# A recurrent block between two FFNs on eight cores: ScalarE functions grouped by channel block, GeLU as one operation, new stage order on TensorE, output weights loaded into freed buffers

## The reference

```python
def rglru_block(h, w_in, conv_w, conv_b, w_a, b_a, w_x, b_x, lam, w_out):
    xb, gate = jnp.split(h @ w_in, 2, axis=-1)
    xb = causal_depthwise_conv(xb, conv_w, conv_b)      # width 4, frames t-3..t
    r = jax.nn.sigmoid(block_diag_linear(xb, w_a, b_a)) # 16 blocks of 64 x 64
    i = jax.nn.sigmoid(block_diag_linear(xb, w_x, b_x))
    log_a = -LRU_C * r * jax.nn.softplus(-lam)
    a = jnp.exp(log_a)
    mult = jnp.sqrt(-jnp.expm1(2.0 * log_a))
    u = mult * (i * xb)
    _, hseq = lax.associative_scan(_lru_combine, (a, u), axis=1)
    y = hseq * jax.nn.gelu(gate)
    return y @ w_out
```

## Time and profile before

| | |
|---|---|
| time before, median of 3 runs | 3065.8 us (2877.21 to 3173.42) |
| the profiled execution | 2881.14 us, its span on the slowest core 2879.6 us |
| spans of the 8 cores in it | 2866.5 to 2879.6 us |
| TensorE, busy share of the span | 91% |
| VectorE / ScalarE / GpSimd | 45% / 28% / 11% |
| table loads of ScalarE | 41, 1283 ns each |

### The profile page before, as it was taken

One profiled execution on the slowest core, in us unless ns is written; L12 is line 12 of the kernel. 1 busy time (PEld: TensorE's weight loads), 2 busy tenths in 40 slices (PEclk: granted clock), 3 DMA queues, 4 the chain that ended last, 5 costly groups with the idle time before them and its releaser, 6 DMA issues.

```text
span 2879.6 us, 31123 instructions; the slowest of 8 cores (2866.5 to 2879.6 us)
## 1 busy us (share of the span) xinstructions
PE 2631.3 (91%) x12224; PEld 1101.3 (38%) x12224; DVE 1282.5 (45%) x2019; ACT 796.7 (28%) x1147; POOL 329.9 (11%) x340
## 2 busy tenths in 40 slices
PE   5999999788888889999998999999677769999999
PEld 1444444333333234444443444444233323444443
DVE  3234434655555451443345234434678734324444
ACT  4110111355565441001114110012377712110100
POOL 0000000011111000000000000000055610000000
PEclk9999999899999989999998999999889979999999
DMA  5412122010001032212212221121011023121213
GB/s 144 77 31 37 30 45 33 8 30 16 16 19 23 15 52 37 37 27 40 45 23 44 37 37 30 30 44 23 4 21 26 2 52 52 30 42 32 37 30 117
DMA packets 56099, 105.88 MB, mean 37 GB/s; under 512 B 4624, under 2 KB 5776, under 8 KB 55952
## 3 DMA queue, kind: packets, MB, share of 16 engines
q0 software_dynamic: 44288, 83.90, 17.7%
q1 hardware_dynamic: 11664, 19.99, 2.3%
HBM read 179.37 MB, written 8.39 MB: 65 GB/s over the span
## 4 chain that ended last, share of the span: by engine, by line
PE 83%; ACT 8%; DVE 5%; issue 1%; DMA 1%; POOL 1%; SPq 0%; ACTq 0%; DVEq 0%; POOLq 0%
PE ps L288 83%; ACT arena L297 6%; DVE arena L300 3%; ACT L297 1%; DVE arena L304 1%; DMA arena<-xT 1%; POOL arena L304 0%; DVE arena L573 0%; DMA arena<-lru_wout 0%; ACT ps L297 0%; DVE arena L718 0%; SPq L326 0%; DVE arena L308 0%; POOL arena L782 0%; DVE arena L311 0%
## 5 line engine op out<-in xcount | busy, mean ns | idle before, releaser
L288 PE MATMUL ps<-arena 128*128 128x512 bf16 (+6 forms) x12224 | 2631.3, 380 | 244.8 <-ACT arena L297 139.4
L288 PEld LDWEIGHTS ps<-arena 128*128 128x128 bf16 (+2 forms) x12224 | 1101.3, 101 | 1774.3 <-issue 275.0
L297 ACT ACTIVATE arena<-ps 128x512 bf16<-128x512 f32 (+5 forms) x680 | 444.9, 661 | 1774.9 <-PE ps L288 1733.7
L304 DVE TENSOR_TENSOR arena<-arena,ps 128x512 bf16<-128x512 bf16 x352 | 242.0, 687 | 956.1 <-PE ps L288 956.1
L300 DVE SCALAR_TENSOR_TENSOR arena<-ps,arena 128x512 f32<-128x512 f32 (+3 forms) x688 | 503.2, 732 | 220.9 <-PE ps L288 219.1
L297 ACT ACTIVATE arena<-arena 128x512 bf16<-128x512 f32 (+4 forms) x338 | 250.1, 756 | 230.0 <-PE ps L288 127.3
L304 POOL TENSOR_TENSOR arena<-arena 128x512 bf16<-128x512 f32 (+2 forms) x112 | 180.6, 1616 | 475.6 <-PE ps L288 266.8
L300 DVE SCALAR_TENSOR_TENSOR arena<-arena,ps 128x512 bf16<-128x512 f32 (+1 forms) x224 | 167.5, 810 | 76.1 <-ACT ps L297 51.5
L439 POOL DMA_DIRECT2D arena<-ffn_win x88 | 62.5, 712 | 1209.0 <-PE ps L288 1208.1
L304 DVE TENSOR_TENSOR arena<-arena 128x512 bf16<-128x512 bf16 (+3 forms) x188 | 87.3, 476 | 94.5 <-ACT arena L297 92.6
L445 POOL DMA_DIRECT2D arena<-ffn_wout x88 | 47.3, 550 | 509.2 <-PE ps L288 508.5
(11 more groups left out here) (20 smaller groups left out, 78.9 us busy)
## 6 DMA issues: line engine op xcount, KB each, us to landing
arena<-ffn_win POOLq DMA_DIRECT2D x88, 512.0 KB, 5.3
arena<-ffn_wout POOLq DMA_DIRECT2D x88, 256.0 KB, 6.5
arena<-xT SPq DMA_DIRECT2D x32, 256.0 KB, 9.5
outT<-arena SPq DMA_DIRECT2D x32, 256.0 KB, 2.9
arena<-attn_win POOLq DMA_DIRECT2D x8, 768.0 KB, 8.5
arena<-lru_win POOLq DMA_DIRECT2D x8, 512.0 KB, 5.4
arena<-bias_tab SPq DMA_DIRECT2D x8, 256.0 KB, 2.9
arena<-attn_wout POOLq DMA_DIRECT2D x8, 256.0 KB, 4.5
```

What stands on the lines that cost most here:

```text
L288: self.P.op("pe", lambda e: e.matmul(out_ap, lhsT, rhs, start=start, stop=stop), reads=reads, writes=[self.ps_t[bank]])
L297: self.P.op("act", lambda e: e.activation(out=out, in_=in_, func=func, **kw), reads=reads, writes=writes)
L304: self.P.op(eng, lambda e: e.tensor_tensor(out=out, in0=in0, in1=in1, op=op), reads=reads, writes=writes)
```

## The change

GeLU becomes one ScalarE operation (`GELU(k)`, function Gelu_apprx_tanh) that reads the gate banks; the Square, one of the Tanh and two VectorE operations of each unit go. The gate projection (`A2`, now `GM(k)`) has two pairs of banks (2,3 and 4,5), and may be issued in halves; `XB` has only banks 0,1. Where `B_rest` handled one unit, the loop now handles both units of a channel block: four Exp in a row, then two Sqrt, and the two GELU a block later beside the Tanh of the next one. The scans and the products with the GeLU come one block later, among the next block's stages. 13 buffers of 128x1024 float32 are dealt out as rings (xc 2, thx 4, Ab 3, tha 4). The GeLU is kept in the norm's scratch and in the unused ends of two weight slots.

At the start, the norm of frame tile 3 is no longer computed before the block, but after `XB(0)`, `GM(0)` and `CONV(0)`. At the end, w_out is loaded in five parts: row 0 early, rows 1 to 4 into weight slots that are done, rows 5 to 7 into two `thx` buffers after the last product of POOL that uses them. The output projection of tile 0 runs rows 0 to 6 for all 8 banks, then row 7 for all; tiles 1 to 3 use four banks in turn. The built program has 33 table loads in place of 41.

```diff
-        if t >= 1:
+        if t >= 1 and not (nn == 4 and t == NT - 1):
             self.rmsnorm_tile(nn, t - 1)
-        if t == NT - 1:
+        if t == NT - 1 and nn != 4:
             self.rmsnorm_tile(nn, t)
...
+        for nm, cnt in (("xc", 2), ("thx", 4), ("Ab", 3), ("tha", 4)):
+            RING[nm] = pool_[k0:k0 + cnt]
...
+        def GELU(k):
+            i = k % 2
+            self.act(gw[i], g2[i], AF.Gelu_apprx_tanh, GB[i], gw_t[i])
...
-            self.act(gw, g2, AF.Square, GB, [Tt["gw"]], scale=0.21145921)
-            self.stt(gw, gw, 1.0, g2, ALU.add, ALU.mult, [Tt["gw"]] + GB, [Tt["gw"]])
-            self.act(gw, gw, AF.Tanh, [Tt["gw"]], [Tt["gw"]], scale=0.7978845608)
-            self.stt(gw, gw, 1.0, g2, ALU.add, ALU.mult, [Tt["gw"]] + GB, [Tt["gw"]])
...
+        XB(0)
+        GM(0)
+        CONV(0)
+        self.rmsnorm_tile(n, 3, 4, 5)
+        BD(0)
+        GM(1, (0,))
+        XB(1)
+        GM(1, (1,))
...
+        for c in range(NCH + 1):
+            u0, u1 = 2 * c, 2 * c + 1
+            if c > 0:
+                GELU(u0 - 2)
+            if 0 < c < NCH:
+                BD(u0)
+            if c > 1:
+                GM(u0 - 1, (1,))
+            if c > 0:
+                GELU(u0 - 1)
+                if c + 2 < NCH:
+                    load_w(c + 2)
+            if c == NCH:
+                break
+            if c == 0:
+                load_out((0,), 0)
+            CONV(u1)
+            if c > 0:
+                SCAN(u0 - 2)
+            BD(u1)
+            MUL1(u0)
+            if c > 0:
+                Y(u0 - 2)
+                SCAN(u0 - 1)
+            MUL1(u1)
+            if c > 0:
+                Y(u0 - 1)
+            if c == NCH - 1:
+                load_out((3, 4), 2)
+            EXP2(u0)
+            EXP2(u1)
+            MIN(u0)
+            EXP1(u0)
+            EXP1(u1)
+            if c + 1 < NCH:
+                XB(u0 + 2)
+                CONV(u0 + 2)
+            MIN(u1)
+            if c > 0:
+                GM(u0)
+                GM(u1, (0,))
+            if c + 1 < NCH:
+                XB(u1 + 2)
+            SQ(u0)
+            MUL2(u0)
+            SQ(u1)
+            MUL2(u1)
+            if c == NCH - 2:
+                load_out((1, 2), 1)
+            if c == NCH - 1:
+                load_out((5, 6), 3)
+                load_out((7,), 4)
+        k0, k1 = nu - 2, nu - 1
+        obank = [0, 1, 6, 7, 2, 3, 4, 5]
+        for c in range(8):
+            omm(0, c, obank[c], range(0, 7))
+        SCAN(k0)
+        Y(k0)
+        SCAN(k1)
+        Y(k1)
+        for c in range(8):
+            omm(0, c, obank[c], range(7, 8))
+            oadd(0, c, obank[c])
```

254 lines of the change are left out of this document (134 added, 120 removed).

## The result

| | before | after |
|---|---|---|
| median of the runs | 2974.67 us (4 runs, 2877.21 to 3173.42) | 2869.02 us (4 runs, 2833.39 to 2943.57) |
| ratio, 95% interval | | 0.9844 [0.9823, 0.9865] |
| the profiled execution | 2881.14 us, span 2879.6 | 2833.39 us, span 2831.8 |
| spans of the 8 cores | 2866.5 to 2879.6 us | 2818.3 to 2831.8 us |

The change makes the kernel 1.56% faster, by an interval that leaves out 1. The profiled execution lost 47.8 us where 38 were forecast. Two of the four runs on either side were disturbed (the cores of a die ran longer at a lower clock) and are left out of the ratio, but not out of the medians.

What follows compares the result with a forecast made beforehand. It took turns between VectorE and POOL to bound the block. Start and block 0 51, six blocks of 28 and tail 37 make 256 against 286.0; with 8 from the projection, 2881.1 - 38 = 2843 us, 80% range 2808 to 2868.

Steps and rivals of the forecast that it cites:

- tail: End of the recurrent block, from the last `XB` to the flowing projection: 37 us (31 to 41).
- projection, before 78.3: Output projection: four banks let TensorE run ahead during the norm, so two 3.11 us gaps go; 8 us saved (5 to 10).
- The mechanism: Steady block: VectorE's scans and `MIN` exclude POOL's operations, 23.2 us a block in queue order; TensorE waits for `CONV`.
- The rival in which the scans run beside POOL: Recurrent block: only `MIN` waits for POOL; 24.3 us a block, 2814 us in all; chance 0.22.
- 26.5 of order and 1.5 of clock: Steady block: 26.5 us by the queues' order with TensorE at full clock, taken as 28 for slower clock after gaps.
- no steady gain: Steady block: 29.3 us, with slow clock after every gap and a tail of 41; 2858 us in all; chance 0.23.
- The block of 24 without turns: Steady block if VectorE were free and `MIN` took 0.7: the chain closes at 23.9 us.
- The clock rival: Recurrent block: TensorE stays at 1.2 GHz throughout, 45 us a block, 2952 us in all, slower by 2.5%; chance 0.05.
- 2068 at full clock, 2075 at half; I take 2071: Start of the recurrent block: trace time for `XB(1)`, making the start 25 us from 2046.3.
- only then come rows 5 and 6: Tail: these w_out rows are issued after both `MUL2` end at 30.2 and land in 5 to 8 us, giving 37.
- The loads of rows 0 to 4 cost nothing: Tail: these w_out loads land beside other work, so they add no time.
- Tables: ScalarE: eight table loads saved, 10 us by the trace or 21 by the skill page, neither shortening the chain.

## Why the prediction was right or wrong, point by point

VectorE's rows that open a `CONV(u1)`, after, give the periods; the first and the last of the eight (the second opens at 2094.21):

```profile
2066.65 1.34 DVE L312 TENSOR_SCALAR arena<-ps,arena 128x1024 f32<-128x1024 f32 x1 [3.87 <-PE ps L289]
...
2259.09 1.34 DVE L312 TENSOR_SCALAR arena<-ps,arena 128x1024 f32<-128x1024 f32 x1 [2.02 <-PE ps L289]
```

The FFN's last matmul ended at 2045.2 (TensorE restarted at 2035.78, 1.2 us earlier than before).

| term | forecast | measured |
|---|---|---|
| start, to the end of `XB(1)` | 25 | 2066.4 - 2045.2 = 21.2 |
| block 0 | 26 | 2094.2 - 2066.65 = 27.6 |
| six blocks | 168 (28 each) | 2259.1 - 2094.2 = 164.9 (27.5 each) |
| tail | 37 | 2291.8 - 2258.9 = 32.9 |
| sum, before 286.0 | 256 | 246.6 |
| projection, before 78.3 | 70 | 70.0 |

- **The step that failed is the price of the two ends.** The start, 25, and the tail, 37, were each 4 us too long, and these two are 8 of the 10 us by which the sum missed the profiled execution. They measured 21.2 and 32.9; the two points on them below say why.
- **The mechanism was right.** What sets the block is the turns of POOL and VectorE, with the scans among them: 3.8 to 4.3 us for a scan beside POOL, `MIN(u0)` 2.77, TensorE waiting for `CONV` and not for ScalarE. The forecast has one order of turns for all blocks, and that order holds in three of the six; in the other three a short operation or POOL pays, as shown above. The rival in which the scans run beside POOL falls by the run without `MUL1`. SBUF — State Buffer of the Trainium skill, "Who interferes with whom", has the rule, and the scans of 2.28 and 4.28 agree; it says too that a `tensor_scalar` can be excluded, in a mode with two ports, and `MIN`'s 2.77 for 0.69 agrees.
- **The steady block, 28 against 27.5.** The block itself gained only 1.1 us on the 28.6 of before, some 7 us over six blocks; most of the 47.8 us is at the ends and in the projection. Its two parts were 26.5 of order and 1.5 of clock. The clock cost 1.7 (5.1 for 3.4), so the order took 25.7. Counted as there, from the end of `XB(u1)` (2203.7), the scans end at 10.0 and 14.3 (forecast 8.7 and 14.65), `MIN(u0)` at 17.0 (17.7), and `XB(u1+2)` starts at 22.3 (23.1). The turns were right within 0.8 us, but for the first scan, which ended 1.3 late, and the order was not the one given: POOL's `tensor_scalar` comes beside the first scan, not behind it, because `load_w` has held POOL until then. The wait of `load_w` was not in the list of turns at all, so that the near hit is in part luck.
- **The rival "no steady gain", 29.3 a block, falls**: 27.5 against 28.6. (The block of 24 without turns is a wrong sum: 13.7, 0.7, 5.3 and 3.4 are 23.1, with the hand-overs some 23.3 and not 23.9. The forecast doesn't rest on it.) The gap of 3.4 us is shorter than the 4.4 that it was priced with.
- **The clock rival falls**: 0.94 over the six blocks, and 1.00 in the half of a block behind the gap of 0.97.
- **The start failed by 4 us.** The step was "2068 at full clock, 2075 at half; I take 2071". The 36 records at 2059.44 took 8.89 us behind gaps of 1.00 and less, at granted clock 1.00; the end of `XB(1)`, 2066.4, is about the full clock's number less the 1.2 by which everything is earlier. Block 0 gave 1.6 of it back, with gaps of 4.53 and 5.53. (Before, "real work begins at 2065.3" was a misreading that the sum doesn't use: TensorE runs 18 matmuls from 2052.01 to 2058.20.)
- **The tail failed by 4 us, in two terms.** The last `MUL2` was forecast to end at 30.2 and ended at 27.4 (2286.34, where the issues begin). The forecast put `MUL1(u0)` behind the first scan; in the last block, which has no `load_w`, POOL ran it ahead of the scan (2263.98 to 2267.5), so that `Y(u0-2)` ended at 13.2 and not at 17.0. From there to the flowing projection it was 5.4 us, not 6.8: the landing was priced from a row with eight loads in flight, and a median load now took 4.4. A third step, "only then come rows 5 and 6", described the order of the change rightly but didn't ask whether the buffers were free before. They were, behind `SCAN(u0-1)`: TensorE stood 11.7 us in two waits for w_out, and the run with the early loads brings 12 us in. "The loads of rows 0 to 4 cost nothing" fits the change, in which the wait that ended last was for rows 5 and 6; issued late, the rows cost 8.4 us.
- **The projection was right**, 8.3 for 8, and the run with two banks gives 10 back, with the two gaps of 3.11.
- **"Tables" was priced rightly at nothing, for GELU wrongly.** The four GeLU operations were counted as busy time saved, 4.9 us of VectorE a block, with no effect on the chain. In the new order they are in the chain: the run with four operations has blocks of 36 us. The forecast never asked what the new order would be with the old GeLU, and so missed that the two parts need each other.

## What to carry to other kernels

Where VectorE and GpSimd share a loop, write their operations into one list of turns, together with every DMA issue that waits for a third engine, and look for the operation that TensorE needs: its wait counts with the whole operation of the other engine ahead of it, so that two minimums of 0.7 us a block were worth 20 us in all, and three operations on one to three columns cost 2 us a block. A function that is merged and an order that is changed are to be priced together, since each alone, as tried, lost time here. When a load is waited for at the end of a phase, ask for each row when its home was free, not when the program got to it.
